# A hybrid attention, mLSTM and SwiGLU layer: five sets of seven products and one plain stretch, with four weight sums formed in memory

## What is computed

```python
proj = h @ w_in[layer]
(q_a, k_a, v_a, q_m, k_m, v_m, o_m, i_m, f_m, g_a, g_m) = jnp.split(proj, split_points, axis=-1)
...
merged = (jax.nn.sigmoid(g_a) * (y_a @ w_out_attn[layer])
          + jax.nn.sigmoid(g_m) * (y_m @ w_out_mlstm[layer]))
x = x + merged @ w_o[layer]
h = rms_norm(x, ffn_norm_g[layer])
x = x + (jax.nn.silu(h @ w_ffn_gate[layer]) * (h @ w_ffn_up[layer])) @ w_ffn_down[layer]
return rms_norm(x, final_norm_g)
```

## Time and profile before

| | |
|---|---|
| median of 3 runs | 377.54 us |
| profiled execution, its own time | 377.2 us |
| span of the profiled execution | 375.4 us |
| granted clock of TensorE, mean | 0.995 |
| TensorE busy | 367.1 us, 98% |
| VectorE busy | 321.5 us, 86% |
| ScalarE busy | 230.7 us, 61% |
| memory read | 73.46 MB |

### The profile page before, as it was taken

The page is one execution under the profiler, slowest core; times in us unless marked ns, Lnnn a source line. Parts: engine busy times, 40 slices in busy tenths (PEclk is TensorE's granted clock), DMA queues, the critical chain, the costliest instruction groups (busy, mean ns, idle before and its releaser), DMA issues.

```text
span 375.4 us, 4744 instructions
## 1 busy us (share of the span) xinstructions
PE 367.1 (98%) x1847; PEld 309.0 (82%) x1847; DVE 321.5 (86%) x372; ACT 230.7 (61%) x267; POOL 41.4 (11%) x41
## 2 busy tenths in 40 slices
PE   7999999999999999999999999999999999999993
PEld 6998888788888888888888888888888888888882
DVE  4989987989867999989769669999999999999525
ACT  5767787676265956645447436955782892878205
POOL 2798020000000104000100000100100100000002
PEclk9999999999999999999999999999999999999998
DMA  8997255945270493899717902794796599360002
GB/s 284 282 296 266 60 182 207 320 143 210 57 281 0 66 345 120 321 353 308 281 55 276 358 39 55 179 384 172 184 359 236 129 308 347 113 248 33 0 2 112
DMA packets 41293, 74.80 MB, mean 199 GB/s; under 512 B 2316, under 2 KB 14648, under 8 KB 41272
## 3 DMA queue, kind: packets, MB, share of 16 engines
q1 hardware_dynamic: 38944, 70.03, 53.2%
q0 software_dynamic: 2112, 4.19, 6.6%
q10 hardware_dynamic: 216, 0.28, 0.2%
HBM read 73.46 MB, written 1.05 MB: 198 GB/s over the span
## 4 chain that ended last, share of the span: by engine, by line
PE 95%; DMA 1%; DVE 1%; issue 1%; POOL 0%; ACT 0%; POOLq 0%; SPq 0%; DVEq 0%; ACTq 0%
PE pp L1685 12%; PE pp L1687 12%; PE pp L1686 12%; PE pa L2069 7%; PE pa L2067 7%; PE pa L2068 7%; PE pp L1676 4%; PE pp L1665 3%; PE pp L1678 2%; PE pa L1676 2%; PE pa L2012 2%; PE pa L2010 2%; PE pa L1685 2%; PE pa L1687 2%; PE pa L2011 2%; PE pa L1686 2%
## 5 line engine op out<-in xcount | busy, mean ns | idle before, releaser
L1088 DVE TENSOR_TENSOR w_lo<-w_raw,w_hi 128x2048 fp32r<-128x2048 f32 x33 | 75.3, 2293 | 10.2 <-ACT w_hi L697 10.1
L970 ACT ACTIVATE w_hi<-w_raw 128x2048 fp32r<-128x2048 f32 x33 | 62.7, 1908 | 24.3 <-DVE w_raw L1536 24.3
L1556 DVE TENSOR_TENSOR w_lo<-w_raw,w_hi 128x2048 fp32r<-128x2048 f32 x33 | 74.6, 2283 | 0.2 <-ACT w_hi L970 0.2
L697 ACT ACTIVATE w_hi<-w_raw 128x2048 fp32r<-128x2048 f32 x33 | 62.6, 1912 | 19.6 <-DMA w_raw<-in_w_in 9.2
L1685 PE MATMUL pp<-w_hi,yT_hi 128*128 128x512 f32 (+1 forms) x104 | 40.5, 390 | 0.0
L1687 PE MATMUL pp<-w_lo,yT_hi 128*128 128x512 f32 (+1 forms) x104 | 40.3, 388 | 0.0
L1686 PE MATMUL pp<-w_hi,yT_lo 128*128 128x512 f32 (+1 forms) x104 | 40.3, 387 | 0.0
L1685 PE MATMUL pp<-w_hi,hT 128*128 128x512 f32 x96 | 38.0, 396 | 0.0
L1687 PE MATMUL pp<-w_lo,hT 128*128 128x512 f32 x96 | 37.4, 390 | 0.0
L1686 PE MATMUL pp<-w_hi,hT 128*128 128x512 f32 x96 | 37.4, 389 | 0.0
L2067 PE MATMUL pa<-w_hi,hT 128*128 128x512 f32 x64 | 24.9, 389 | 0.0
(11 more groups left out here) (341 smaller groups left out, 780.5 us busy)
## 6 DMA issues: line engine op xcount, KB each, us to landing
w_raw<-in_w_in SPq DMA_DIRECT2D x20, 1024.0 KB, 5.4
w_raw<-in_w_ffn_gate SPq DMA_DIRECT2D x11, 1024.0 KB, 8.9
w_raw<-in_w_ffn_up SPq DMA_DIRECT2D x11, 1024.0 KB, 8.5
w_raw<-in_w_ffn_down SPq DMA_DIRECT2D x11, 1024.0 KB, 7.9
w_raw<-in_w_o SPq DMA_DIRECT2D x4, 1024.0 KB, 5.3
x_sb<-in_w_ffn_gate POOLq DMA_DIRECT2D x3, 1024.0 KB, 9.3
w_raw<-in_w_out_attn SPq DMA_DIRECT2D x2, 1024.0 KB, 9.8
w_raw<-in_w_out_mlstm SPq DMA_DIRECT2D x2, 1024.0 KB, 5.2
```

What stands on the lines that cost most here:

```text
L697: nc.scalar.activation(w_hi[:, slot_of(c), :], early_raw(c), ACT.Copy).then_inc(hi_ready, 1)
L970: nc.scalar.activation(w_hi[:, slot_of(c), :], form_raw(name, p), ACT.Copy).then_inc(hi_ready, 1)
L1088: nc.vector.tensor_tensor(w_lo[:, slot_of(c), :], early_raw(c), w_hi[:, slot_of(c), :].bitcast(F32), ALU.subtract).then_inc(lo_ready, 1)
L1556: nc.vector.tensor_tensor(w_lo[:, slot_of(c), :], form_raw(*FORM[c]), w_hi[:, slot_of(c), :].bitcast(F32), ALU.subtract).then_inc(lo_ready, 1)
```

## The change

The plain stretches go from three to one and the sets from four to five (`SETS`, `PLAIN`); the columns are the same 2816. SyncE issues four copies from memory to memory, into a new internal tensor `formed`: two behind the load of chunk 8, two behind that of chunk 17. GpSimd adds a second block (or the finished T1) to each by an adding transfer: T1 of set 0 ahead of its wait for the mLSTM weights, T3 of set 0 behind those masks, T2 of set 0 right behind the gate's own adding transfer, T1 of set 1 behind the reciprocal root `lnr`. These four sums are then loaded like chunks; T2 of set 0 goes to `x_sb` and waits for the last transposes of the normed input (`turned` 16), with the later loads behind it in SyncE's list. The sets' splits run 4 (3 in set 0) chunks ahead, not 5. B11 of set 0 takes the place of NG 1 among the early chunks, T1 of set 0 that of NU 1. The activations' sums move ahead of the split of T1. Some semaphores are merged.

```diff
-SETS = 4
-PLAIN = 3
+SETS = 5
+PLAIN = 1
 SUMS = ("T1", "T2", "T3", "T4")
+AHEAD_FORMED = {("T1", 0): ("B12", "B11"), ("T3", 0): ("B22", "B12"), ("T2", 0): ("B22", ("T1", 0)), ("T1", 1): ("B12", "B11")}
+STORED = {form: n for n, form in enumerate(AHEAD_FORMED)}
...
-C_SETS = C_FFN + 4
+C_SETS = C_FFN + 3
...
-            place("B12", p, "T1")
+            place("T1" if ("T1", p) in STORED else "B12", p, "T1")
...
-    first = AT["B11", 0]
-    ahead = RING if c < first else LEAD
+    ahead = LEAD - 1 if c <= AT["B11", 0] else LEAD - 2 if c < AT["T4", 0] else LEAD - 1
     return min(max(c + ahead, split_to(c - 1)), C_FFN + len(AT) - 1)
...
+            def form_copy(name, p):
+
+                n, src = STORED[name, p], ffn_source(AHEAD_FORMED[name, p][0], p)
+                if n >= 2:
+                    sp.wait_ge(formed_copied[n % 2], 16 * (n // 2))
+                sp.dma_start(formed[n].rearrange("p (k n) -> p k n", k=4), src).then_inc(formed_copied[n % 2], 16)
...
+                if c == 8:
+                    form_copy("T1", 0)
+                    form_copy("T3", 0)
+                if c == 17:
+                    form_copy("T2", 0)
+                    form_copy("T1", 1)
...
             for (name, p), (buf, value, freed, count) in LANDED.items():
                 src = ffn_source(name, p)
+                if (name, p) in STORED:
+                    sp.wait_ge(formed_grown, 16 * (STORED[name, p] + 1))
                 sp.wait_ge({"lo": lo_ready, "sum": w_summed, "normed": normed, "num": num_done}[freed], count)
                 sp.dma_start(as_source(raw_of(buf), src), src).then_inc(chunk_loaded[buf], 16)
+                if (name, p) == ("B22", 0):
+
+                    src = ffn_source("T2", 0)
+                    sp.wait_ge(formed_grown, 16 * (STORED["T2", 0] + 1))
+                    sp.wait_ge(turned, 16)
+                    sp.dma_start(as_source(x_sb[:, :], src), src).then_inc(t2_loaded, 16)
...
+            def form_grow(name, p):
+
+                second, n = AHEAD_FORMED[name, p][1], STORED[name, p]
+                dst = formed[n].rearrange("p (k n) -> p k n", k=4)
+                src = ffn_source(second, p) if isinstance(second, str) else ffn_source(*second)
+                pool.wait_ge(formed_copied[n % 2], 16 * (n // 2 + 1))
+                if n:
+                    pool.wait_ge(formed_grown, 16 * n)
+                nc.gpsimd.dma_start(dst.rearrange("p k n -> k p n"), src.rearrange("p k n -> k p n"), accum_op=ALU.add
+                                    ).then_inc(formed_grown, 16)
+
+            form_grow("T1", 0)
             pool.wait_ge(w_exp_done, 2 * H_M)
...
+            form_grow("T3", 0)
             pool.wait_ge(lo_ready, GM["T2"] + 1)
             pool.wait_ge(gm_summed, 3)
             src = gm_source("B21")
             nc.gpsimd.dma_start(as_source(region_b[:, :], src), src, accum_op=ALU.add).then_inc(gm_grown, 16)
 
+            form_grow("T2", 0)
             pool.wait_ge(var_set, H_M)
             link(nc.gpsimd.tensor_scalar(lnv[:, :], mv[:, :, 1], EPS, None, ALU.add))
             nc.gpsimd.tensor_tensor(lnr[:, :], lnv[:, :], minus_half[:, :], ALU.pow).then_inc(lnr_set, 1)
+            form_grow("T1", 1)
             rsqrt(2)
...
             plain(0, 0)
             plain(0, 1)
-            plain(1, 0)
-            plain_turn(0)
-            plain(1, 1)
-            down("dN", 0)
-            plain_turn(1)
-            plain(2, 0)
-            plain(2, 1)
             for p in range(SETS):
```

More of the change, by code:

```diff
@@ L66, in places @@
 def places():
-    names = [("NG", 0), ("NU", 0), ("NG", 1), ("NU", 1), ("dN", 0), ("NG", 2), ("NU", 2)]
+    names = [("NG", 0), ("NU", 0)]
     for p in range(SETS):
-        before, after = (("dN", 1), ("dN", 2)) if p == 0 else (("dA", p - 1), ("dB", p - 1))
-        names += [("B11", p), ("T1", p), ("T2", p), ("B22", p), before, ("T3", p)]
-        names += [after, ("B21", p), ("T4", p)] if p + 1 < SETS else [("B21", p), ("T4", p), after]
+        before, after = ([], [("dN", 0)]) if p == 0 else ([("dA", p - 1)], [("dB", p - 1)])
+        names += [("B11", p), ("T1", p), ("T2", p), ("B22", p)] + before + [("T3", p)]
+        names += after + [("B21", p), ("T4", p)] if p + 1 < SETS else [("B21", p), ("T4", p)] + after
     names += [("dA", SETS - 1), ("dB", SETS - 1)]
@@ L77, with sum_count @@
 AT = places()
-C_SETS = C_FFN + 4
+C_SETS = C_FFN + 3
 def lo_place(name, p):
     return 2 * AT[name, p]
-def sum_count(name, p):
-    return 3 * p + SUMS.index(name) + 1
 def grown(name, p):
     return name == "T4" and p + 1 < SETS
+SUMMED = [(name, p) for p in range(SETS) for name in SUMS if not grown(name, p) and (name, p) not in STORED]
+def sum_count(name, p):
+    return SUMMED.index((name, p)) + 1
 def sums_ahead(name, p):
-    return {"T1": ("T1", "T2"), "T2": ("T3",), "B21": ("T4",) if p + 1 == SETS else ()}.get(name, ())
+    sums = {"T1": ("T1", "T2"), "T2": ("T3",), "B21": ("T4",)}.get(name, ())
+    return [part for part in sums if (part, p) in SUMMED]
 FORM = {c: form for form, c in AT.items()}
@@ L142, in landings @@
             place("B11", p, "T3")
-            place("B12", p, "T1")
+            place("T1" if ("T1", p) in STORED else "B12", p, "T1")
             place("B22", p, "B22")
-        elif name not in SUMS + ("B22",):
+        elif (name, p) == ("T1", 0):
+            place("T1", p, "T1")
+            place("B22", p, "B22")
+        elif name not in SUMS + ("B22",) or (name, p) == ("T3", 0):
             place(name, p, name)
@@ L333, in form_raw @@
                 return x_sb[:, :]
-            return raw_of(LANDED[{"T1": "B12", "T3": "B11"}.get(name, name), p][0])
+            if name in SUMS and (name, p) not in STORED:
+                name = {"T1": "B12", "T3": "B11"}[name]
+            return raw_of(LANDED[name, p][0])
         def plain_banks(n):
@@ L479, in build @@
         w_grown = sem("w_grown")
+        t2_loaded = sem("t2_loaded")
+        formed_copied = [sem(f"formed_copied{n}") for n in range(2)]
+        formed_grown = sem("formed_grown")
         part_kept = sem("part_kept")
@@ L940, in _, with form_hi @@
                 ins.then_inc(ym_hi_set, 1)
+            def form_hi(c):
+                name, p = FORM[c]
+                if grown(name, p):
+                    act.wait_ge(w_grown, 16 * (p + 1))
+                elif (name, p) == ("T2", 0):
+                    act.wait_ge(t2_loaded, 16)
+                elif (name, p) in SUMMED:
+                    act.wait_ge(w_summed, sum_count(name, p))
+                else:
+                    act.wait_ge(chunk_loaded[LANDED[name, p][0]], LANDED[name, p][1])
+                act.wait_ge(chunk_used, c - RING + 1)
+                nc.scalar.activation(w_hi[:, slot_of(c), :], form_raw(name, p), ACT.Copy).then_inc(hi_ready, 1)
             split_hi(C_WO)
@@ L1039, in _ @@
                     nc.scalar.activation(gate1, pa[:, own_bank(p), :], ACT.Silu).then_inc(set_silu, 1)
-                elif name == "dN" and p == 0:
-                    plain_hi(1)
                 for n in split_behind(c):
@@ L1557, in form_lo @@
                                         w_hi[:, slot_of(c), :].bitcast(F32), ALU.subtract).then_inc(lo_ready, 1)
+            norm(3, gain_ffn)
+            turn_lo(7, 1, (pp[:, 0, :], pp[:, 1, :]))
+            dve.wait_ge(h_copied, 1)
+            nc.vector.tensor_tensor(sum1, pp[:, 0, :], sum2, ALU.subtract).then_inc(h_summed, 1)
+            nc.vector.tensor_tensor(sum3, sum4, pp[:, 0, :], ALU.subtract).then_inc(h_summed, 1)
+            dve.wait_ge(h_summed, 1)
+            nc.vector.tensor_tensor(sum2, sum1, sum4, ALU.subtract).then_inc(h_summed, 1)
+            dve.wait_ge(h_summed, 3)
+            nc.vector.tensor_tensor(sum4, pa[:, 1, :], sum2, ALU.add).then_inc(h_summed, 1)
+            form_lo(C_SETS)
             def plain_product(n):
@@ L2048, in down @@
                 for t in tiles:
-                    if name == "dN" and p == 0 and t == 1:
-                        pe.wait_ge(plain_prod, 2)
                     for k in range(2):
```

118 lines of the change are left out of this document (41 added, 77 removed).

## The result

The changed kernel takes 428.75 us (median of 4 runs, 427.84 to 430.43) where the kernel before takes 377.62 (377.19 to 378.04): 1.136 times as long, 95% interval 1.132 to 1.140. The profiled execution has a span of 426.3 us.

The account below looks back on a forecast made before the run. TensorE, 98% busy, was taken as the bound: 377.2 - 2.7 (12 matmuls) + 3.0 (stall at `turn_merged(0)`) + 0.2 (stall in the sets) = 377.7 us, range 374.6 to 380.2.

Parts of the forecast that it names:

- 12 matmuls fewer, 2.7 us: Gate and up products: a fifth set of 84 matmuls replaces two plain stretches of 2 x 48, saving 2.7 us.
- VectorE's share and the stock: SwiGLU sets: VectorE gains 4.5 us, later sets stay balanced, stock shrinks 2.7 us, margin 1.3 us, no stall.
- Rival D: Sets 0 and 1: VectorE becomes the bound, TensorE waits 1 to 2 us, no merge stall, 376.0 us; chance 0.10.
- B: Rival at the merge: adds yield to loads or cost like a load, gain stands, 374.7 to 375.2 us; chance 0.32.
- I put 0.2 us of stall there, between 0 and 1.5: At T2 and `set_lo` of set 1, where VectorE meets TensorE within a few tenths: 0.2 us of stall.
- Copies at 0: Copies behind chunks 8 and 17: 0.37 us each on SyncE's list, in stretches with little traffic.
- I take 5.9, the nearest row: Price of one memory-to-memory add, from rows for adds into SBUF: 5.9 us, between 3 and 9.
- The reckoning by volume: Set 1's T1 add: from 150.4 the engines owe 11.9 us of transfers, so chunk 30's load lands about 162.3.
- rival C: Adds dearer than 5.9 us delay chunk 26, then chunk 30; at 7.4 us, 379.2 to 380.7 us; chance 0.18.
- The first two adds at 0: Set 0's T1 and T3 adds, around the mLSTM masks: cost 0, with 1.5 us as upper bound for T3's.
- just covered: 0: T2's add, first output product: chunk 26's load lands near 144.5, latest allowed 145.4, so no cost.
- T1's add of set 1, 3.0 us at `turn_merged(0)`: Before the merge: the add makes chunk 30's `w_o` load 3.2 us late, idling TensorE 3.0 us.

Follow-up runs that it names:

- the version with quiet adds: Changed kernel with adds partition outermost, T3's load ahead of T2's, adds of T3, T2 and set 1's T1 moved to 82 and 98 us: 375.96 us, 0.9953 of before.
- the order with T3's load first: Changed kernel without copies and adds, with T2's load behind T3's in SyncE's list instead of ahead: 375.79 us, 0.9954 of before.
- the order alone: Changed kernel with neither copies nor adds, the four sums replaced by unsummed weight blocks: 377.61 us, 1.0002 of before.
- the kernel with no adds: Changed kernel with its four copies and without its four adds in memory: 379.23 us, 1.0045 of before.

## Why the prediction was wrong

The steps, in the prediction's own order.

- **12 matmuls fewer, 2.7 us: right.** TensorE has 1835, and most of this gain shows as soon as the rest is mended: the version with quiet adds is 1.7 us faster, the order with T3's load first 1.8. Of the missing 1.0 us in the first, 0.2 is left at T2 of set 1; the rest was not followed up.
- **VectorE's share and the stock: right.** No set behind set 1 has a stall in any run, and once the loads are in order TensorE waits at most 0.3 us for VectorE in the whole block. Rival D falls; B, that the gain stands, holds for the adds in their quiet places, not in the change's. GpSimd's masks were covered, as said: they start at 53.17, before at 53.09.
- **Set 0, "I put 0.2 us of stall there, between 0 and 1.5": the place right, the reason and the size wrong.** TensorE stood 1.8 us there in the order alone, 2.6 with the copies. I checked that T3, dN and B21 come in time behind T2's load, but not the adding transfer that GpSimd issues behind them, T4's: 13.2 us to landing. It was the step "T2's load holds up T3, dN and B21 behind it ... wanted over 217, later than 212.4" that looked at the loads and left the add out.
- **Copies at 0: nearly.** 1.6 us in the kernel with no adds, of which 0.9 is a second wait of TensorE there (0.88 us beside the 1.76), where that same add lands at 224.3, not 222.8. The version with quiet adds, which has the copies, is within 0.2 us of the one with T3's load first, which hasn't.
- **"I take 5.9, the nearest row", with 9 as upper bound: the step that failed.** The rows were for a pattern with the partition outermost, and the change's has k outermost. I looked at the ends of the transfer (memory or SBUF) and not at its shape, which stands in the diff. The reckoning by volume behind it has all transfers share all the engines; a load beside such an add took 12.3 us where I had 10.0. For the shape of the rows the number was good: a rate of 185 GB/s is 5.7 us for an MB. For the shape of the change it was 24.4 alone and 35 to 41 in the kernel, and rival C, "dearer than 5.9 us", was drawn up to 7.4 only. The rate of the Trainium skill's HBM Reference, section Specifications (TRN2), which I weighed by volume, was no help: volume wasn't what costs. The rule that mattered stands on another page of the Trainium skill, the one named above: four engines out of sixteen, which with the 5.9 us of the earlier trace rows is an estimate of 4 x 5.9 = 24 us.
- **The first two adds at 0, T2's "just covered: 0": wrong at the real price.** The first alone costs 12.2 us. With partition outermost the three cost 1.6 together (380.84 against 379.23), T2's at rival C's place: chunk 26's load lands at 145.5, just past the 145.4 that I had named as the latest.
- **T1's add of set 1, 3.0 us at `turn_merged(0)`: the mechanism right, the size too small.** With partition outermost it costs 6.05. The two loads of `w_o` took 11.2 and 9.7 us beside it, where I had 10.0 and 8.5. The first four transposes waited 2.8 us, nearly the 3.0; missing were the second four, which wait for the next merge (1.4 us), and the clock, which falls to 0.77 behind the stop. "Nothing later gives them back" was right; that something later adds to them I hadn't counted.

With the adds at the price that I had given them the change is at 386.9, also outside my range. So there are two errors. One is the pattern, 41.9 us where the change has its adds (59 us in the quiet version, so its price hangs on the place too). The other is 9.2 us (386.9 - 377.7), which the runs split: the order 2.6 (377.6 against 377.5 - 2.7 + 0.2), the copies 1.6, three adds 1.6, T1's add of set 1 3.0 more than its 3.0, and 0.3 between the two executions' own times of before. These are differences of single runs in part, and add up but for 0.1. None of these is large; I had put all of them at 0 to 0.2, T1's add apart, each with a margin read off one load or one engine at a time.

## What to carry to other kernels

Read the access pattern of a transfer before its price: the outermost index says over how many of the 16 DMA engines it is dealt, and a pattern with 4 values there took 24.4 us instead of 9.3, and a load wholly beside it 12.1 to 12.3 instead of 5.1 (8.1 beside the add with partition outermost). A row of the trace prices a transfer of its own shape only. Here an adding transfer that nobody was waiting for was free in a stretch with few loads, and in a chain without slack it cost its delay and the clock behind it; before moving one, list what stands behind it on the issuing engine, because in GpSimd's list slow adds delayed the gate's own from 126.4 to 165.0.

## What the hardware showed that I had not expected

A transfer of half the size took as long as the whole (24.2 and 24.4 us), because half as many rows were dealt out by 2 outermost values instead of 4. SyncE's queue deals a copy out in the same way as GpSimd's. With partition outermost, an add with both ends in memory costs 9.3 us to landing, one into SBUF 8.7: memory as the destination is hardly dearer. And a stop of TensorE cost more than its length: the granted clock of the next 5 us was 0.50 behind the stops of 9.1 and 3.1 us in the changed kernel, 0.53 behind 5.1, 0.64 behind 10.0, and 0.77 behind the 2.8 and 1.4 us with partition outermost.
